# Two heads in one value product of the first attention, a gate unit in its middle, and the meta levels beside the substitution

## The chip, the cores and the metric

One core of a Trainium2 chip runs the whole program. The time is the device time of one execution in microseconds (us), the median of several. TensorE (PE in the profile) multiplies, with the loading of its stationary operand in a row of its own (PEld); VectorE (DVE), ScalarE (ACT) and GpSimd (POOL) do the elementwise work; SyncE (SP) and the queue of GpSimd start transfers. Each engine takes its instructions strictly in the order in which they are written, and semaphores tie the engines together.

## What is computed

Two transformer blocks over 256 tokens of 1024 features. The first prepends 16 meta tokens, projects them once, and runs two branches side by side: a gated delta rule (GDN, 8 heads, chunks) and a sparse attention (DSA, 8 query heads on 2 key heads, the 64 best keys of each query). Both are gated, merged, projected, and followed by an MLP. The second block has a modulated differential attention, a Fourier branch and 16 routed experts. The change touches only these two pieces of the first block:

```python
# GDN, per head and chunk: a triangular inverse, and what it is applied to
A = tril(einsum(k*beta, k) * decay, -1)
Tm = solve_triangular(A + I, I)
attn = einsum(q, k) * decay;  q_dec = q * exp(gc);  g_last = exp(gc[-1])
# DSA, per block of 128 queries and head
p = softmax(where(chosen and causal, q @ k.T * 128**-0.5, -inf))
o = p @ v
merged = sigmoid(gate_a) * (y_gdn @ w_bg) + sigmoid(gate_b) * (y_dsa @ w_bd)
```

## The kernel before

Everything is written by hand, engine by engine, in raw order; no scheduler moves anything. Weights stream in units of 1 MB (128 x 8 x 256 fp32) through a ring of six slots (`ring`, `weight_order`). A dense product is `split_tiles`: ScalarE copies the unit to a rounded type (`w_high`, two buffers, `highs`, L1475), VectorE subtracts that from the unit (`ring_low`, `lows`, L1923), and TensorE does 48 matmuls of 256 columns (L670, L671, L676). `after_unit(kind, u)` stands in the programs of ScalarE and of VectorE where they prepare the unit two places behind the one named: its copy may start only when the unit before it in the same `w_high` buffer has been used. Eight PSUM banks are taken in rotation (`take`); a bank is taken again when its reader has freed it.

**The head loop and the substitution (GDN).** For each of 8 heads TensorE fills three banks: `GB` (the cumulated decay, and beta spread over columns), `KQ` (k·k and k·q) and `TR` (transposes of k and v). VectorE's `decay_args` (L2025) writes the exponents, ScalarE exponentiates them (L1588, L1589) into `scr[:, h % 2]`, and VectorE's `decay_use` masks them (L2035), copies the last column to `egl` (L2036), makes `attn` (L2039), `low` (L2040, L2043) and the decayed q (L2041). ScalarE then makes `k_tail` and `v_beta` from `TR` (L1596, L1597). `decay_args(h)` waits until `TR` of head h-2 is freed by ScalarE, and the exponents of head h-1 are used behind it. Between the heads stand the four meta levels, an inverse of one 128x128 system by doubling: per level one product P (`level_p`, L787), a copy out by ScalarE (`product_out`), one or two products Q and QT (`level_q`, L797, L802) and an update by VectorE (`update_inverse`, L2052 to L2057), each waiting for the one ahead. GpSimd masks the input of each level (L1409) and clears `inv` and `invT` (L1401, L1402) when the last `GB` is filled.

Behind the last head VectorE runs the substitution: four transposes (L2082), 15 steps of two small operations (L2093, L2095), four scalings and eight transposes back (L2107), after which `blocks_ready` lets the remaining twelve levels start on TensorE. TensorE meanwhile has units `mod` 6 and 7 and the two fillers `gz` 0 and 1 (L632, 64 matmul instructions).

**The first attention (DSA).** 16 items `ATT`, first the eight heads of query block 0 (144 keys), then those of block 1 (272 keys). Per item n: logits on TensorE (`att_logits`, L950), mask and maximum on VectorE (L2256, L2258), exponent on ScalarE (L1678), reciprocal and scaling on VectorE (L2265, L2267), transposes on TensorE (`att_transpose`, L958), copy out by ScalarE (L1687, L1688), value product on TensorE (`att_values`, L632, 128 columns, one matmul for each tile of keys), and copy out (L1458) with, for block 1, the rounded copy (L1694) and its remainder on VectorE (L2270). TensorE's order is logits n+1, transposes n-1, values n-3. VectorE's order in item n is mask and maximum of n, then reciprocal and scaling of n-1. Ahead of the transposes stands gate unit `gate_b` 0, and behind the attention the rest alternates, `bd` 0, `gate_b` 1, `bd` 1, `gate_b` 2, ...

## Time and profile before

| what | value |
|---|---|
| three runs | 1255.33, 1258.56, 1259.81 us, median 1258.56 |
| the profiled execution | 1259.38 us, its span 1257.6 us |
| TensorE busy | 1191.4 us, 95% of the span, mean granted clock 0.976 |
| VectorE, ScalarE, GpSimd busy | 667.8, 502.1, 83.9 us |
| the chain that ended last | TensorE 87%, VectorE 9%, ScalarE 2% |

The span is the time from the first to the last recorded instruction; 1.8 us of the execution lie outside it. A row of the timeline says when an instruction began, how long it took, and in brackets how long its engine had sat idle and who ended that. Instructions of one engine overlap in their first and last part, so the next may begin before the one ahead has ended; what a step costs on an engine is the distance between two starts.

### The profile page before, as it was taken

The page shows a single profiled execution, that of the slowest core. Times are in us where ns is not written, and L with a number is a line of the kernel's source. Part 1 is how long each engine was busy: PE and PEld are TensorE (multiplying, and loading weights), DVE is VectorE, ACT ScalarE, POOL GpSimd, SP SyncE. Part 2 cuts the span into 40 slices and gives each one's busy share as a digit, 9 for nine tenths or more (in the row PEclk, how much of TensorE's full clock was granted, in tenths as well). Part 3 has the DMA queues.
Part 4 walks back from the last instruction along what each step waited for, and adds up shares of the span by engine and source line. Part 5 has one row for each costly group of instructions (what it writes and reads, how often), then busy time and mean ns, then how long its engine had stood idle before and what let it go on. Part 6 is the DMA issues. An engine that isn't in the chain of part 4 may idle for free.

```text
span 1257.6 us, 21686 instructions
## 1 busy us (share of the span) xinstructions
PE 1191.4 (95%) x9068; PEld 1027.9 (82%) x9068; DVE 667.8 (53%) x1161; ACT 502.1 (40%) x809; POOL 83.9 (7%) x80
## 2 busy tenths in 40 slices
PE   7999779999899989999998999999899899999996
PEld 6998669998879969999997889966799866666665
DVE  5776685487966565664646332576556441122223
ACT  4775322554355455554344222466533301011112
POOL 2541113000000000000000000000001100000000
PEclk8999889999999999999998999999999899999999
DMA  9546030153422655554554522300865989999980
GB/s 363 189 146 243 13 135 1 68 172 130 163 106 101 239 198 212 191 188 165 184 186 154 196 101 71 132 33 6 326 234 219 387 365 420 420 420 420 420 346 34
DMA packets 36206, 254.61 MB, mean 202 GB/s; under 512 B 4048, under 2 KB 4192, under 8 KB 5904
## 3 DMA queue, kind: packets, MB, share of 16 engines
q1 hardware_dynamic: 33552, 237.83, 49.1%
q0 software_dynamic: 2560, 15.42, 3.1%
q8 instruction: 72, 1.18, 0.4%
q14 instruction: 22, 0.18, 0.0%
HBM read 252.19 MB, written 1.05 MB: 201 GB/s over the span
## 4 chain that ended last, share of the span: by engine, by line
PE 87%; DVE 9%; ACT 2%; issue 2%; DMA 0%; DVEq 0%; ACTq 0%
PE bank L1255 14%; PE bank L676 12%; PE bank L670 12%; PE bank L671 12%; PE bank L632 9%; PE bank L1016 5%; PE bank L1065 4%; PE bank L1023 2%; PE bank L714 1%; PE bank L1274 1%; PE bank L689 1%; PE bank L787 1%; PE bank L802 1%; DVE ring_low L1923 1%; DVE rB L1904 1%
## 5 line engine op out<-in xcount | busy, mean ns | idle before, releaser
L1923 DVE TENSOR_TENSOR ring_low<-ring,w_high 128x2048 fp32r<-128x2048 f32 x104 | 237.9, 2289 | 175.5 <-ACT w_high L1475 175.2
L1475 ACT ACTIVATE w_high<-ring 128x2048 fp32r<-128x2048 f32 x104 | 199.4, 1917 | 311.7 <-PE bank L676 222.3
L670 PE MATMUL bank<-nT_high,w_high 128*128 128x256 f32 (+1 forms) x448 | 115.3, 296 | 0.0
L670 PEld LDWEIGHTS bank<-nT_high,w_high 128*128 128x128 f32 x448 | 85.0, 190 | 2.6 <-issue 2.4
L1255 PE MATMUL bank<-more,xs 128*64 128x256 f32 x768 | 84.5, 379 | 0.0
L670 PE MATMUL bank<-hcl,w_high 128*128 128x256 f32 (+1 forms) x288 | 81.9, 316 | 2.2 <-DVE hcl L2367 2.2
L1255 PEld LDWEIGHTS bank<-more,xs 128*64 128x64 f32 x768 | 55.1, 137 | 29.8 <-issue 2.9
L671 PE MATMUL bank<-hcl,w_high 128*128 128x256 f32 (+1 forms) x288 | 79.4, 307 | 0.0
L670 PE MATMUL bank<-nMs,w_high 128*128 128x256 f32 x256 | 65.2, 292 | 2.0 <-DVE nMs L2312 2.0
L671 PE MATMUL bank<-nT_low,w_high 128*128 128x256 f32 (+1 forms) x272 | 65.5, 282 | 0.0
L671 PE MATMUL bank<-nMs,w_high 128*128 128x256 f32 x256 | 64.8, 291 | 0.0
L1016 PE MATMUL bank<-up,w_high 128*128 128x256 f32 x512 | 64.2, 283 | 0.0
L1016 PEld LDWEIGHTS bank<-up,w_high 128*128 128x128 f32 x512 | 62.5, 192 | 0.1
L670 PEld LDWEIGHTS bank<-hcl,w_high 128*128 128x128 f32 x288 | 55.2, 192 | 7.7 <-issue 4.7
L676 PE MATMUL bank<-nT_high,ring_low 128*128 128x256 f32 (+1 forms) x448 | 59.1, 284 | 1.1 <-DVE ring_low L1923 1.1
L671 PEld LDWEIGHTS bank<-hcl,w_high 128*128 128x128 f32 x288 | 55.2, 192 | 3.5 <-issue 1.0
L676 PEld LDWEIGHTS bank<-nT_high,ring_low 128*128 128x128 f32 x448 | 56.2, 188 | 1.5 <-DVE ring_low L1923 1.5
L670 PEld LDWEIGHTS bank<-nMs,w_high 128*128 128x128 f32 x256 | 51.2, 200 | 2.6 <-issue 2.5
L671 PEld LDWEIGHTS bank<-nT_low,w_high 128*128 128x128 f32 x272 | 52.0, 191 | 1.5 <-issue 1.4
L671 PEld LDWEIGHTS bank<-nMs,w_high 128*128 128x128 f32 x256 | 51.2, 200 | 0.0
L1871 ACT ACTIVATE yb_high<-bank,gate_slot 128x512 fp32r<-128x512 f32 x18 | 12.4, 687 | 82.0 <-PE bank L1255 76.0
L676 PE MATMUL bank<-hcl,ring_low 128*128 128x256 f32 (+1 forms) x288 | 44.4, 307 | 0.0
(542 smaller groups left out, 2490.9 us busy)
## 6 DMA issues: line engine op xcount, KB each, us to landing
ring<-stream SPq DMA_DIRECT2D x163, 1024.0 KB, 4.9
more<-stream SPq DMA_DIRECT2D x60, 1024.0 KB, 16.4
more<-stream POOLq DMA_DIRECT2D x10, 1024.0 KB, 15.3
c<-constants_one SPq DMA_DIRECT2D x1, 1653.0 KB, 16.2
qc<-h_in SPq DMA_DIRECT2D x4, 272.0 KB, 3.8
c<-constants_two POOLq DMA_DIRECT2D x1, 1056.0 KB, 9.4
beside<-stream POOLq DMA_DIRECT2D x1, 1024.0 KB, 12.2
hT<-h_in POOLq DMA_DIRECT2D x1, 1024.0 KB, 5.9
```

Of the source, the lines that this page charges most:

```text
L632: last = nc.tensor.matmul(dst, lhs, rhs, start=(i == 0), stop=(i == len(pairs) - 1))
L670: nc.tensor.matmul(into[j], w, high_x(k), start=first, stop=False, skip_group_check=True)
L671: nc.tensor.matmul(into[j], w, low_x(k), start=False, stop=False, skip_group_check=True)
L676: last = nc.tensor.matmul(into[j], low_w[:, k, j * 128:(j + 1) * 128], high_x(k), start=False, stop=(k == KT - 1), skip_group_check=True)
L689: last = nc.tensor.matmul(dst[rows, 0:UNIT_COLS], silu_c[:, k, :], by_k(s)[:, k, :], start=(k < 4), stop=(k >= 4))
L714: last = nc.tensor.matmul(psum[banks.at[name]][:, 0:n], ones, src[:, k, :], start=(k == 0), stop=(k == KT - 1), skip_group_check=True)
L1016: nc.tensor.matmul(dst[:, j * SEQ:(j + 1) * SEQ], high_w[:, k, j * 128:(j + 1) * 128], up[:, kg * KT + k, part, :], start=(kg == 0 and k = ...
L1023: last = nc.tensor.matmul(dst[:, j * SEQ:(j + 1) * SEQ], low_w[:, k, j * 128:(j + 1) * 128], up[:, kg * KT + k, 0, :], start=False, stop=( ...
L1065: return nc.tensor.matmul(dst[tp][:, j * 256:(j + 1) * 256], hcl[:, 2 * tp + part, k, j * 128:(j + 1) * 128], w[:, k, :], start=first, sto ...
L1255: last = nc.tensor.matmul(dst[rows, :], stationary[:, k, rows], w[j][:, k, :], start=(k == 0), stop=(k == n_k - 1))
L1475: A(w_high[:, d % 2, :], ring[:, s, :], ACT.Copy).then_inc(high_ready, 1)
L1923: TT(ring_low[:, s, :], ring[:, s, :], w_high[:, d % 2, :], sub).then_inc(low_ready, 1)
```

## The change

In the GDN part, the four meta levels leave the head loop on TensorE, ScalarE and VectorE. TensorE does them after the heads, between `mod` 6, `mod` 7 and quarters of the two fillers (`quarter`), ScalarE's `product_out` 0 to 3 stand among the copies of these, and VectorE's updates 0 to 2 stand inside the substitution (behind its first transposes, behind step 9, behind the last step). The copy to `egl` and the decayed q move from VectorE's `decay_use` to GpSimd, which does them for all eight heads behind its second level mask and ahead of clearing `inv` and `invT`.

In the DSA part the transposes of heads 2p and 2p+1 go into one bank (for block 1 into two), ScalarE copies them out as a pair, one value product has 256 columns, and y is copied out and split by pairs. TensorE does the values of pair p at n = 2p + 4. `prob` has four buffers. The order of the weights becomes `gate_b` 0, `gate_b` 1, `bd` 0, `bd` 1, `gate_b` 2, ...; gate unit 1 is multiplied at n = 8, in the middle of the attention, and `after_unit` of gate units 0 and 1 (which prepare `bd` 0 and `bd` 1) stand at n = 5 and n = 13 in both ScalarE's and VectorE's loop.

```diff
-    for u in range(4):
+    order += [("gate_b", 0), ("gate_b", 1), ("bd", 0), ("bd", 1)]
+    for u in range(2, 4):
         order += [("gate_b", u), ("bd", u)]
...
-                if h % 2 == 1:
-                    level_p(h // 2)
-                elif h >= 2:
-                    level_q(h // 2 - 1)
...
             mod_unit(6)
+            level_p(0)
             mod_unit(7)
-            level_q(META_LEVELS - 1)
+            level_q(0)
+            quarter(0, 0)
+            quarter(0, 1)
+            level_p(1)
+            quarter(0, 2)
+            level_q(1)
+            quarter(0, 3)
+            level_p(2)
+            quarter(1, 0)
+            level_q(2)
+            quarter(1, 1)
+            level_p(3)
+            quarter(1, 2)
+            level_q(3)
+            quarter(1, 3)
...
+                if n == 2:
+                    for h in range(H):
+                        pool.wait_ge(decay_exp_ready, h + 1)
+                        pool.wait_ge(*banks.full_when[("KQ", h)])
+                        nc.gpsimd.tensor_copy(egl[:, 2 * h:2 * h + 2], scr[:, h % 2, 256:512].rearrange("p (a b) -> p a b", b=128)[:, :, 127])
+                        nc.gpsimd.tensor_tensor(qc[:, h, META:T], qc[:, h, META:T], scr[:, h % 2, 256:512], mul).then_inc(gpsimd_product, 1)
...
                 step(TT(split(dt, 128), split(dt, 128), over(upper, 2), mul))
-                step(CP(egl[:, 2 * h:2 * h + 2], split(scr[:, h % 2, 256:512], 128)[:, :, 127]))
...
-                step(TT(qc[:, h, META:T], qc[:, h, META:T], scr[:, h % 2, 256:512], mul))
...
-                done(("ao", n), group(dst[:, 0:128], [(av[0:m, i, g * 128:(g + 1) * 128], probT[0:m, n % 2, i * 128:(i + 1) * 128])
+                done(("ao", p), group(dst[:, 0:256], [(av[0:m, i, g * 128:(g + 1) * 128], probT[0:m, p % 2, i, :])
...
-                if n == 0:
-                    second_gate(0)
+                if n % 8 == 0 and n < len(ATT):
+                    second_gate(n // 8)
                 if 1 <= n <= len(ATT):
                     att_transpose(n - 1)
-                if n >= 3:
-                    att_values(n - 3)
+                if n >= 4 and n % 2 == 0:
+                    att_values((n - 4) // 2)
...
+                if n == 5 or n == 13:
+                    after_unit("gate_b", n // 8)
```

The last two added lines stand in ScalarE's loop behind everything else of item n, and in VectorE's behind the maximum of item n and ahead of the reciprocal of item n-1.

On VectorE, in the attention around items 4 to 6, before (the sixth item of block 0 begins with the second `lmask` row):

```order
L2256 SCALAR_TENSOR_TENSOR lmask<-bank,bias 128x144 [waits bank_full1,pexp_ready]
L2258 TENSOR_REDUCE stat<-lmask 128x1 [waits bank_free1]
L2265 RECIPROCAL stat<-stat 128x1 [waits pexp_ready]
L2267 TENSOR_SCALAR prob<-prob,stat 128x144 [waits dve_step]
L2256 SCALAR_TENSOR_TENSOR lmask<-bank,bias 128x144 [waits bank_full4,pexp_ready]
L2258 TENSOR_REDUCE stat<-lmask 128x1 [waits bank_free4]
L2265 RECIPROCAL stat<-stat 128x1 [waits pexp_ready]
L2267 TENSOR_SCALAR prob<-prob,stat 128x144 [waits dve_step]
```

and in the changed kernel:

```order
L2304 SCALAR_TENSOR_TENSOR lmask<-bank,bias 128x144 [waits bank_full0,pexp_ready]
L2306 TENSOR_REDUCE stat<-lmask 128x1 [waits bank_free0]
L2315 RECIPROCAL stat<-stat 128x1 [waits pexp_ready]
L2317 TENSOR_SCALAR prob<-prob,stat 128x144 [waits dve_step]
L2304 SCALAR_TENSOR_TENSOR lmask<-bank,bias 128x144 [waits bank_full2,pexp_ready]
L2306 TENSOR_REDUCE stat<-lmask 128x1 [waits bank_free2]
L1970 TENSOR_TENSOR ring_low<-ring,w_high 128x2048 [waits high_ready]
L2315 RECIPROCAL stat<-stat 128x1 [waits pexp_ready]
L2317 TENSOR_SCALAR prob<-prob,stat 128x144 [waits dve_step]
L2304 SCALAR_TENSOR_TENSOR lmask<-bank,bias 128x144 [waits bank_full4,pexp_ready]
L2306 TENSOR_REDUCE stat<-lmask 128x1 [waits bank_free4]
```

A subtraction `ring_low` of a whole weight unit has come between the maximum of item 5 and the reciprocal of item 4; it waits for ScalarE's rounded copy of the unit. The same stands in item 13.

On GpSimd, behind the masks of the first levels, before:

```order
L1409 TENSOR_TENSOR masked<-metas,c 128x128
L1409 TENSOR_TENSOR masked<-metas,c 128x128 [waits bank_full1] x2
L1401 MEMSET inv 128x2048 [waits bank_full0]
L1402 MEMSET invT 128x2048
L1411 TENSOR_TENSOR masked<-low,c 128x512 [waits bank_full2,bank_free0]
L1411 TENSOR_TENSOR masked<-low,c 128x512 [waits bank_full3]
```

and in the changed kernel (two of the eight heads, then the clearing):

```order
L1435 COPY egl<-scr 128x2 [waits bank_full6,decay_exp_ready]
L1436 TENSOR_TENSOR qc<-qc,scr 128x256
L1435 COPY egl<-scr 128x2 [waits bank_full1,decay_exp_ready]
L1436 TENSOR_TENSOR qc<-qc,scr 128x256
L1438 MEMSET inv 128x2048 [waits bank_full0]
L1439 MEMSET invT 128x2048
L1446 TENSOR_TENSOR masked<-metas,c 128x128 [waits bank_full4,bank_free0]
L1446 TENSOR_TENSOR masked<-metas,c 128x128 [waits bank_full0]
```

The copy to `egl` and the product with `qc` stand once for each head ahead of the clearing of `inv` and `invT`, and the masks of meta levels 2 and 3 behind it.

On TensorE, between the last head and the first of the remaining levels, before:

```order
L787 MATMUL bank<-metas,masked 128x128 [waits bank_free3,bank_free7,masked_ready]
L689 MATMUL bank<-ring,silu_c 32x256 [waits bank_free4,unit_loaded0]
L689 MATMUL bank<-ring,silu_c 32x256 x7
L689 MATMUL bank<-ring,silu_c 32x256 [waits bank_free5,unit_loaded1]
L689 MATMUL bank<-ring,silu_c 32x256 x7
L802 MATMUL bank<-metas,prod 128x128 [waits bank_free6,bank_free3]
L632 MATMUL bank<-nT,ring 128x256 [waits bank_free7,unit_loaded2]
L632 MATMUL bank<-nT,ring 128x256 x15
L632 MATMUL bank<-nT,ring 128x256 [waits bank_free0,unit_loaded3]
L632 MATMUL bank<-nT,ring 128x256 x15
```

and in the changed kernel, from `mod` 6 to the products of level 1:

```order
L690 MATMUL bank<-ring,silu_c 32x256 [waits bank_free3,unit_loaded0]
L690 MATMUL bank<-ring,silu_c 32x256 x7
L788 MATMUL bank<-c,masked 128x128 [waits bank_free4,masked_ready]
L690 MATMUL bank<-ring,silu_c 32x256 [waits bank_free5,unit_loaded1]
L690 MATMUL bank<-ring,silu_c 32x256 x7
L803 MATMUL bank<-c,prod 128x128 [waits bank_free6,bank_free4]
L834 MATMUL bank<-nT,ring 128x256 [waits bank_free7,unit_loaded2]
L834 MATMUL bank<-nT,ring 128x256 x7
L788 MATMUL bank<-metas,masked 128x128 [waits bank_free0,bank_free6,masked_ready]
L834 MATMUL bank<-nT,ring 128x256 x4
L798 MATMUL bank<-prod,metas 128x128 [waits bank_free1,bank_free0]
L803 MATMUL bank<-metas,prod 128x128 [waits bank_free2]
```

Level 0 and 1 of the meta system stand between the modulation units and the quarters of the fillers; two more levels follow in the same way.

## Rows read from the trace of the kernel before

**Rows 1.** The page: the span.

```profile
span 1257.6 us, 21686 instructions
```

**Rows 2.** Windows: stretch, its length, busy us and instructions of each engine, granted clock, DMA.

```profile
183.00:187.00 4.00, 3.93 (x18) 3.96 (x19) 1.42 (x2) 0.67 (x2) 1.18 (x2) 0.50 0.02 4
...
360.20:387.00 26.80, 25.38 (x149) 17.94 (x148) 18.88 (x64) 19.81 (x83) 0.00 (x0) 1.00 0.11 40
```

**Rows 3.** Timeline of VectorE in the head loop, heads 1 and 2.

```profile
127.21 0.61 DVE L2025 TENSOR_SCALAR scr<-bank,tok 128x128 f32<-128x128 f32 x2 [2.30 <-PE bank L810]
...
128.61 0.41 DVE L2040 TENSOR_TENSOR low<-bank,scr 128x256 f32<-128x256 f32 x1
...
130.23 0.61 DVE L2025 TENSOR_SCALAR scr<-bank,tok 128x128 f32<-128x128 f32 x2 [0.40 <-ACT v_beta L1597]
```

**Rows 4.** Timeline of TensorE: a wait of a meta level.

```profile
142.00 0.49 PE L797 MATMUL bank<-prod,metas 128*128 128x128 f32 x2 [1.98 <-ACT prod L1458]
```

**Rows 5.** Timeline of GpSimd: a product of the convolution, and the clearing.

```profile
68.00 2.56 POOL L1395 TENSOR_TENSOR qc<-qc,scr 128x272 f32<-128x272 f32 x1 [1.35 <-ACT scr L1515]
72.75 0.77 POOL L1395 TENSOR_TENSOR qc<-qc,scr 128x272 f32<-128x272 f32 x1 [2.18 <-ACT scr L1515]
...
153.73 1.80 POOL L1401 MEMSET inv<- 128x2048 f32 x1 [16.87 <-PE bank L810]
155.47 1.80 POOL L1402 MEMSET invT<- 128x2048 f32 x1
```

**Rows 6.** Timeline of VectorE: a level's update, and the last two heads.

```profile
152.28 0.29 DVE L2056 TENSOR_TENSOR metas<-metas,bank 128x128 f32<-128x128 f32 x1 [1.26 <-PE bank L797]
...
154.30 0.41 DVE L2035 TENSOR_TENSOR scr<-scr,c 128x256 f32<-128x256 f32 x1
154.64 2.66 DVE L2036 COPY egl<-scr 128x2 f32<-128x2 f32 x1
...
160.20 0.41 DVE L2043 TENSOR_TENSOR low<-low,bank 128x256 f32<-128x256 f32 x1
```

**Rows 7.** Timeline of TensorE beside and behind the substitution.

```profile
163.09 14.01 PE L632 MATMUL bank<-nT,ring 128*128 128x256 f32 x64
183.07 3.75 PE L787 MATMUL bank<-inv,masked 128*128 128x128 f32 x16 [5.98 <-issue]
...
188.60 1.06 PE L787 MATMUL bank<-inv,masked 128*128 128x128 f32 x8
```

**Rows 8.** Timeline of TensorE in the attention: one item of each block.

```profile
365.32 0.41 PE L950 MATMUL bank<-ak,aq 128*128 128x144 f32 x2
...
366.69 0.41 PE L950 MATMUL bank<-ak,aq 128*128 128x144 f32 x2
...
376.39 0.62 PE L950 MATMUL bank<-ak,aq 128*128 128x272 f32 x2
376.85 0.49 PE L958 MATMUL bank<-c,prob 128*16 128x128 f32 x3
377.27 1.12 PE L632 MATMUL bank<-probT,av 16*128 16x128 f32 x6
378.23 0.62 PE L950 MATMUL bank<-ak,aq 128*128 128x272 f32 x2
```

**Rows 9.** Timeline of VectorE in the attention.

```profile
356.28 2.29 DVE L1923 TENSOR_TENSOR ring_low<-ring,w_high 128x2048 fp32r<-128x2048 f32 x1
...
365.84 0.31 DVE L2256 SCALAR_TENSOR_TENSOR lmask<-bank,bias 128x144 f32<-128x144 f32 x1 [0.25 <-PE bank L950]
...
377.12 0.44 DVE L2256 SCALAR_TENSOR_TENSOR lmask<-bank,bias 128x272 f32<-128x272 f32 x1 [0.54 <-PE bank L950]
...
378.14 0.36 DVE L2267 TENSOR_SCALAR prob<-prob,stat 128x272 f32<-128x272 f32 x1
```

**Rows 10.** Timeline of ScalarE: the rounded copies of y and of a unit.

```profile
377.37 0.42 ACT L1694 ACTIVATE y_dsa_high<-y_dsa 128x256 fp32r<-128x256 f32 x1
...
387.95 1.90 ACT L1475 ACTIVATE w_high<-ring 128x2048 fp32r<-128x2048 f32 x1
```

More of the change, by code:

```diff
@@ L822, in _, with quarter @@
                 done(("TR", h), last)
-                if h % 2 == 1:
-                    level_p(h // 2)
-                elif h >= 2:
-                    level_q(h // 2 - 1)
+            placed = {}
+            def quarter(u, q):
+                if q == 0:
+                    placed[u] = unit("gz", u), take(("gz", u))
+                (s, cnt), dst = placed[u]
+                j, half = divmod(q, 2)
+                for k in range(half * KT // 2, (half + 1) * KT // 2):
+                    last = nc.tensor.matmul(dst[:, j * SEQ:(j + 1) * SEQ], by_k(s)[:, k, j * 128:(j + 1) * 128], nT[:, k, META:T],
+                                            start=(j == 0 and k == 0), stop=(k == KT - 1), skip_group_check=True)
+                if q == 3:
+                    last.then_inc(unit_used[s], 1)
+                    banks.full_when[("gz", u)] = (unit_used[s], cnt)
             mod_unit(6)
+            level_p(0)
             mod_unit(7)
-            level_q(META_LEVELS - 1)
-            for kind, u in FILLERS:
-                s, cnt = unit(kind, u)
-                dst = take((kind, u))
-                for j in range(2):
-                    last = group(dst[:, j * SEQ:(j + 1) * SEQ], [(by_k(s)[:, k, j * 128:(j + 1) * 128], nT[:, k, META:T]) for k in range(KT)])
-                last.then_inc(unit_used[s], 1)
-                banks.full_when[(kind, u)] = (unit_used[s], cnt)
+            level_q(0)
[13 more added lines that the diff above has]
+            quarter(1, 3)
             for n in range(META_LEVELS, len(LEVEL_ITEMS)):
@@ L1599, in _ @@
                             ins.then_inc(free(("TR", g)), 1)
-                if h >= 2 and h % 2 == 0:
-                    product_out(h // 2 - 1)
             evac_mod(6)
+            product_out(0)
             evac_mod(7)
-            for u in range(2):
-                gz_out(u)
+            product_out(1)
+            product_out(2)
+            gz_out(0)
+            product_out(3)
+            gz_out(1)
             for n in range(META_LEVELS, len(LEVEL_ITEMS)):
@@ L1656, in second_gate @@
                     emptied(act, ("bg", u + 2))
-                A(gate[:, u % 2, :], full(act, ("gate_b", u))[:, :], ACT.Copy if u == 0 else ACT.Sigmoid).then_inc(free(("gate_b", u)), 1)
+                A(gate[:, u % 2, :], full(act, ("gate_b", u))[:, :], ACT.Copy if u < 2 else ACT.Sigmoid).then_inc(free(("gate_b", u)), 1)
             first_gate(0)
@@ new lines, in _ @@
+                    A(prob[:, n % 4, 0:nkeys(qt)], lmask[:, n % 2, 0:nkeys(qt)], ACT.Exp, bias=stat[:, n % 2, 0:1],
+                      accum_out=stat[:, n % 2, 1:2]).then_inc(pexp_ready, 1)
+                if n >= 3 and n % 2 == 1 and n < len(ATT) + 3:
+                    p = (n - 3) // 2
+                    qt, h = ATT[2 * p]
+                    bank = full(act, ("pt", p))
+                    if p >= 2:
+                        act.wait_ge(*banks.full_when[("ao", p - 2)])
+                    if qt == 0:
+                        step(A(probT[0:META, p % 2, 0, :], bank[0:META, 256:512], ACT.Copy))
+                        A(probT[:, p % 2, 1, :], bank[:, 0:256], ACT.Copy).then_inc(free(("pt", p)), 1)
+                    else:
+                        A(probT[:, p % 2, 1:3, :], bank[:, :].rearrange("p (a b) -> p a b", b=256), ACT.Copy).then_inc(free(("pt", p)), 1)
+                        A(probT[0:META, p % 2, 0, :], full(act, ("pt_meta", p))[0:META, 0:256], ACT.Copy).then_inc(free(("pt_meta", p)), 1)
@@ L2260, in _ @@
                     after_unit("bg", 3)
+                if n == 5 or n == 13:
+                    after_unit("gate_b", n // 8)
                 if n >= 1:
```

105 lines of the change are left out of this document (57 added, 48 removed).

## The prediction

> **What bounds the kernel.** I read the page first, for the span [rows 1] and for TensorE, which is busy for almost all of it. A change can therefore gain in two ways: less work on TensorE, or less of the little that it waits. So I went to the two stretches that the diff touches, by windows and then by the timelines of each engine. In the attention, 360.2 to 387.0, TensorE has 25.4 of 26.8 us of work at the full granted clock [rows 2]: it is the bound there. In the head loop it waits for ScalarE's copy of a meta level's product, 1.98 us at 142.00, one of three such waits [rows 4]. Behind the loop VectorE alone sets the pace: from the end of its last `low` at 160.61 [rows 6] to the first of the remaining levels at 183.07, before which TensorE had sat idle for 5.98 us [rows 7].
>
> **The head loop.** Where no level stands between, a head takes 3.02 us (VectorE's `decay_args` at 127.21 and at 130.23, the second released by ScalarE's `v_beta`) [rows 3]. The reader is to see a ring: exponents on VectorE, `low` 1.40 behind them, ScalarE's four copies, the next exponents. The changed loop is this ring alone. Of what moves to GpSimd, the product with q stands behind `low` and off the ring, so it saves nothing; the small copy stands inside, but the operation behind it has to await the mask's end in any case, so I count 0.1. Six rings of 2.92 behind 127.21 put the exponents of head 7 at 127.21 + 6 x 2.92 = 144.7. The use of head 6 (0.53 until it begins, then 1.5) and that of head 7 (1.55) end at 148.3. Against 160.61 that is 12.3.
>
> **GpSimd's part.** For each head a copy of two columns and a product of 256, for which the convolution's product of 272 columns shows 0.77 alone and 2.56 where it met VectorE [rows 5]. I take 0.77, plus at most 0.3 for the copy, which fits in 2.92; it starts some 1.4 behind the exponents, when VectorE is at operations that read PSUM. Only the last head has no exponents of a later one ahead of it, so there VectorE's mask (L2035) meets the product: 0.4. Behind it the clearing comes at once, 3.6 us. A price for that stands in rows 6: the small copy took 2.66 us because it arrived within the clearing [rows 5] and was served at its end. If the mask of head 7 were held like that, it would cost 3.6. But L2035 at 154.30, wholly within the same clearing, took its ordinary 0.41 [rows 6]. I take 0.4 and keep 3.6 as the far end.
>
> The Trainium skill ("SBUF — State Buffer", section "Who interferes with whom") says that a VectorE instruction with two SBUF inputs contends with a GpSimd one that reads SBUF, not with one that only writes, and that a copy in a two-port mode contends with either. By that rule the mask would be held by the product and not by the clearing. The copy at 154.64 and the mask at 154.30 agree.
>
> **Levels beside the substitution.** VectorE gets three updates more, each two operations of 0.29 with a wait between [rows 6]: 3 x 0.57 = 1.7. The substitution itself stays 22.5 (160.61 to 183.07). TensorE's work beside it is the fillers (14.0), the two modulation units (3.3) and some 2 for the levels, plus one round trip through ScalarE of about 2 at level 0: done 21 to 24 after 144.5, when VectorE still has 4 or 5 to go. So these waits are covered; if they weren't, the last filler would end later than VectorE, which takes another 5. The sum: 12.3 - 0.4 - 1.7 = **10.2 less**, ends 6.5 (clearing holds the mask) and 12 (updates hidden, nothing met). Everything behind it (levels, scan, dense units) is bound by TensorE or by VectorE's own chain and moves along; no unit is waited for there, since the stream runs ahead.
>
> **The attention: work saved.** In block 1 an item takes 1.84: logits 0.46, transposes 0.42, values 0.96 [rows 8]; in block 0 it takes 1.37. A matmul instruction of 256 columns costs 14.01 / 64 = 0.219 [rows 7], and a product is two of them (six for three tiles [rows 8]). A pair's values cost 6 x 0.219 = 1.31 in place of 1.92, and in block 0 4 x 0.219 = 0.88 in place of about 1.5. Over 4 + 4 pairs: 4.8 less.
>
> **Given back to the chain.** From the start of an item's logits VectorE begins 0.73 later (376.39, 377.12) and ends scaling the item before at 378.50 [rows 8, 9]: the transposes can start 2.1 behind the logits. Before, TensorE had 0.46 + 0.42 + 0.96 + 0.46 = 2.30 in between, so the chain was just hidden. Now values come at every second item only; in the item without them there are 0.46 + 0.42 + 0.46 = 1.34, and TensorE waits 0.7. In block 0, with 0.52 from logits to VectorE [rows 8, 9], it is 0.8. I lay the items out by these numbers: waits of 0.4 and 0.8 in block 0, three of 0.7 in block 1, the rest covered by the gate unit in the middle or the tail; 3.3, of which 0.3 was there before. Net of the two paragraphs: 1.8 less. Gate unit 1 costs what it did (5.8), only earlier.
>
> **The conversions in the middle.** This is the term that I weigh most. Before, the attention held no conversion but the one in item 1 (2.29 at 356.28 [rows 9], under gate unit 0's matmuls), and the next (1.90 at 387.95 [rows 10]) ran under `bd` 0. Now ScalarE does one behind everything of items 5 and 13, and VectorE's subtraction waits for it ahead of the reciprocal of the item before. What stands behind it on VectorE is the scaling of `prob` 4 (or 12), which TensorE's next transposes need; behind those nothing of TensorE can pass. TensorE has one logits product to do and then idles: the exponent (0.4), two pair copies (0.5), the copy of y (0.3), 1.90, 2.25 and the reciprocal and scaling (0.4) make 5.8 from VectorE's maximum (the small ones estimated from the same timeline); without the insertion 0.8 would pass until the transposes. The stall at item 5 is 5.0. At item 13 the copies are longer (0.5, 0.5, 0.3, 0.4, and 0.5 for the rounded copy of a pair, which was 0.42 for one head [rows 10]): 5.5. Of the 10.5 I let 0.9 be saved in shorter waits next to them: 9.6 more. What would hide it is a dense unit on TensorE; gate unit 1 stands at item 8, three items behind the first stall and five ahead of the second. If that cover were there, the term would be nothing.
>
> **The clock.** After the 5.98 idle, the first 16 matmuls took 3.75 us at a granted 0.50, the lower level, where 8 take 0.9 later [rows 2, 7]: 1.9 lost. Two stalls of 5 us should do likewise. Some of it falls in the chain's waits; I take 1.5 each, 3 in all, ends 0 and 4.
>
> **Sum.** -10.2 - 1.8 + 9.6 + 3.0 = +0.6. The attention with gate unit 1, 26.8 + 5.8, becomes 43.4. The profiled execution of before (1259.4, span 1257.6) lies 0.8 above the median; on the median the sum gives 1258.6 + 0.6 = 1259.2, and I say **1259.5**.
>
> **Rivals.**
> 1. *Faster: the stalls at items 5 and 13 don't show.* This would be if VectorE and ScalarE stood items ahead of TensorE. Then 12.6 go away: 1247. Against it, one logits product is all that TensorE gives ahead, and `lmask` has two buffers; the row at 377.12 follows its logits at once. Chance 0.09.
> 2. *The clearing holds the last head's mask*, 3.6 of the gain: 1262.8. The copy's 2.66 speaks for it, the mask's 0.41 against. 0.10.
> 3. *The half clock lasts longer* than after the idle row, through the four or five items behind each stall, where nearly all is on TensorE: 2 more each, 1263.5. 0.10.
> 4. *Slower: GpSimd becomes the bound of the head loop.* If its copy and product take more than the ring's 2.92 (the product alone 2.56 as at 68.00 [rows 5], the copy 0.7 or more), ScalarE's exponents of head h wait for the product of h-2 and the loop takes GpSimd's pace; it decides from 3.7 on, where 7 x 0.8 = 5.6 are lost: 1265 and more. Against it, at 68.00 it met a subtraction of 2.29, and in the loop the longest two-input operation takes 0.41. 0.08. The other side of the page's rule, that each product and each mask of a head stop one another, is this rival in small: 0.4 a head, 3 in all, within the range.
>
> The forecast, about equal sums, has the remaining 0.63. A measurement of this kernel can tell about 0.5%, 6.3 us, from no change. Faster by more is rival 1, 0.09, and a little of the forecast's spread, 0.10 in all; slower is rival 4 and the joint upper ends, 0.12; within is 0.78. The range takes in rivals 2 and 3 and, below, a gain of 12 with a clock that costs nothing: 1254 to 1265.
>
> **What would show it.** GDN: `decay_args` of the heads about 2.9 apart, L2043 of head 7 near 148.5, the first of the remaining levels near 173, three updates inside the substitution. VectorE's mask of head 7 at 0.4 or at 4 tells rival 2; GpSimd's product at 0.8 or 2.5 tells rival 4. Attention: two idle rows of TensorE of 5.0 and 5.5 ended by VectorE's `prob`, each behind a `w_high` and a `ring_low`; waits of 0.7 in every second item; value products in rows of 0.88 and 1.31; a granted clock of 0.50 behind each stall. I am wrong if the stretch from `gate_b` 0's last matmul to `bd` 0's first is under 38 or over 46, or if the GDN gain is under 7.

## The result and the profile after

The changed kernel takes **1266.89 us** (median of 9 runs, 1262.19 to 1269.55), the kernel before 1258.56 (7 runs, 1255.33 to 1259.81): ratio 1.0064, 95% interval 1.0048 to 1.0080. It is slower by some 8 us, where 1259.5 and a range up to 1265 were forecast. The profiled spans are 1265.0 and 1257.6 [rows 1]: 7.4 us, which the account below has to give. Runs that a second, slower condition of the chip disturbed are left out of every median and ratio here.

**The GDN part gained.** VectorE in the changed kernel: the exponents of heads 1, 2 and 7, the mask and `low` of head 7, and the substitution (start, duration, engine, line, operation, idle time before it and who ended that).

```profile
127.54 0.61 DVE L2072 TENSOR_SCALAR scr<-bank,tok 128x128 f32<-128x128 f32 x2 [2.42 <-PE bank L811]
...
130.48 0.61 DVE L2072 TENSOR_SCALAR scr<-bank,tok 128x128 f32<-128x128 f32 x2 [0.76 <-ACT v_beta L1636]
...
145.19 0.61 DVE L2072 TENSOR_SCALAR scr<-bank,tok 128x128 f32<-128x128 f32 x2 [0.76 <-ACT v_beta L1636]
...
147.29 0.44 DVE L2082 TENSOR_TENSOR scr<-scr,c 128x256 f32<-128x256 f32 x1
...
148.56 0.42 DVE L2088 TENSOR_TENSOR low<-low,bank 128x256 f32<-128x256 f32 x1
...
160.21 0.22 DVE L2139 TENSOR_TENSOR state<-state,root 128x55 f32<-128x55 f32 x1
160.70 1.14 DVE L2139 TENSOR_TENSOR state<-state,root 128x48 f32<-128x48 f32 x1
```

Heads 1 to 7 now begin 2.94 us apart (forecast: 2.92), heads 2 to 7 each released by ScalarE's `v_beta`; the last `low` starts at 148.56 where it stood at 160.20 [rows 6]. The mask of the last head, at 147.29, took 0.44.

GpSimd at the same place, and TensorE where the remaining levels begin:

```profile
146.59 0.19 POOL L1435 COPY egl<-scr 128x2 f32<-128x2 f32 x1 [2.08 <-ACT scr L1628]
146.73 0.73 POOL L1436 TENSOR_TENSOR qc<-qc,scr 128x256 f32<-128x256 f32 x1
147.39 1.80 POOL L1438 MEMSET inv<- 128x2048 f32 x1
...
160.69 1.09 POOL L1448 TENSOR_TENSOR masked<-low,c 128x512 f32<-128x512 f32 x1 [4.31 <-PE bank L788]
```

```profile
173.60 3.56 PE L788 MATMUL bank<-inv,masked 128*128 128x128 f32 x16 [5.19 <-issue]
```

The levels begin at 173.60, 9.47 earlier than at 183.07 [rows 7]; 10.2 was forecast. A part of the missing 0.7 stands in the rows: GpSimd's mask at 160.69 reads two SBUF operands, and VectorE's subtraction of the substitution that began with it took 1.14, where the same 48 columns took 0.21 before (at 171.54). The two traces can be compared here because their head loops begin at nearly the same place (exponents of head 0 at 124.30 and 124.52); in most other executions of this study that place is 121.9 to 122.0, so the position of one row in two traces tells a gain only to some 2.5 us, and distances within a trace tell it better: from there to the first of the levels 58.8 before and 49.1 now. The gain arrives unspent at the attention, whose first logits start at 350.53 instead of 360.20.

**The attention lost more than that.** TensorE in the changed kernel, from the first logits behind gate unit 0 (the matmuls of the gate units left out):

```profile
350.53 0.41 PE L970 MATMUL bank<-ak,aq 128*128 128x144 f32 x2
350.77 0.38 PE L985 MATMUL bank<-c,prob 128*16 128x128 f32 x2
350.99 0.41 PE L970 MATMUL bank<-ak,aq 128*128 128x144 f32 x2
352.14 0.38 PE L985 MATMUL bank<-c,prob 128*16 128x128 f32 x2 [0.74 <-DVE prob L2317]
...
353.38 0.38 PE L985 MATMUL bank<-c,prob 128*16 128x128 f32 x2 [0.61 <-DVE prob L2317]
...
354.25 0.39 PE L985 MATMUL bank<-c,prob 128*16 128x128 f32 x2 [0.24 <-DVE prob L2317]
354.56 2.25 PE L633 MATMUL bank<-probT,av 16*128 16x256 f32 x4
356.61 0.69 PE L970 MATMUL bank<-ak,aq 128*128 128x144 f32 x2
361.90 0.59 PE L985 MATMUL bank<-c,prob 128*16 128x128 f32 x2 [4.61 <-DVE prob L2317]
...
373.96 1.32 PE L633 MATMUL bank<-probT,av 16*128 16x256 f32 x4
375.12 0.62 PE L970 MATMUL bank<-ak,aq 128*128 128x272 f32 x2
...
379.33 0.49 PE L985 MATMUL bank<-c,prob 128*16 128x128 f32 x3
379.65 0.62 PE L970 MATMUL bank<-ak,aq 128*128 128x272 f32 x2
381.03 0.50 PE L985 MATMUL bank<-c,prob 128*16 128x128 f32 x3 [0.75 <-DVE prob L2317]
381.46 1.75 PE L633 MATMUL bank<-probT,av 16*128 16x256 f32 x6
383.05 0.62 PE L970 MATMUL bank<-ak,aq 128*128 128x272 f32 x2
389.03 0.80 PE L985 MATMUL bank<-c,prob 128*16 128x128 f32 x3 [5.37 <-DVE prob L2317]
```

What VectorE did in the first of the two long gaps, with the release by ScalarE's rounded copy of the unit:

```profile
359.06 2.29 DVE L1970 TENSOR_TENSOR ring_low<-ring,w_high 128x2048 fp32r<-128x2048 f32 x1 [4.30 <-ACT w_high L1512]
361.27 0.16 DVE L2315 RECIPROCAL stat<-stat 128x1 f32<-128x1 f32 x1
361.46 0.29 DVE L2317 TENSOR_SCALAR prob<-prob,stat 128x144 f32<-128x144 f32 x1
```

The same stretch in windows (length; busy us and instructions of TensorE, its weight loads, VectorE, ScalarE, GpSimd; granted clock; DMA):

```profile
350.53:354.80 4.27, 2.68 (x19) 1.87 (x18) 3.38 (x14) 2.50 (x10) 0.00 (x0) 0.99 0.65 232
354.80:368.70 13.90, 9.29 (x28) 6.17 (x28) 6.07 (x16) 5.75 (x15) 0.00 (x0) 0.51 0.01 5
368.70:388.90 20.20, 13.46 (x82) 10.12 (x80) 8.37 (x22) 9.13 (x22) 0.00 (x0) 1.00 0.16 53
388.90:395.70 6.80, 6.67 (x20) 4.30 (x20) 3.70 (x12) 2.98 (x8) 0.00 (x0) 0.50 0.00 0
```

Both stalls are there, 4.61 and 5.37 (forecast 5.0 and 5.5), each behind a `ring_low` that waited for its `w_high`. The reader is to see two things that the forecast did not have. The value product of a pair takes 1.16 us from start to start in block 0 (373.96 to 375.12) and 1.59 in block 1 (381.46 to 383.05), not 0.88 and 1.31. And the half clock begins at about 354.8, 2.5 us before the first stall, and lasts nearly 14 us (the stall of 4.61 is inside it); with the second stretch of it, it is 20.7 us of the 48.3 from 350.53 to the first matmul of `bd` 0 at 398.83. Before, the same work took 26.84 + 5.8 = 32.6. The loss of 15.7 here is 6.0 more than the 9.67 gained ahead of it, and the span ends 7.4 later.

One saving is smaller and easy to overlook. From the start of an item's transposes to what follows them, TensorE takes 0.42 in block 1 when a value product follows [rows 8] and 0.31 in block 0 (365.64 to 365.95 before), but 0.32 and 0.22 when logits follow (379.33 to 379.65, 350.77 to 350.99). Fourteen such steps led to a value product before, seven do now: 0.6 saved in all.

### The profile page after: what moved, and what is told of

It is laid out like the page before. It is cut to its first block, busy times and chain, and to the rows that moved or that the text cites. A ratio compares the mean times of both kernels' runs of the same rounds, so it can differ in the third digit from the quotient of the medians.

```text
span 1265.0 us, 21561 instructions
## 1 busy us (share of the span) xinstructions
PE 1193.2 (94%) x9028; PEld 1027.4 (81%) x9028; DVE 662.8 (52%) x1141; ACT 501.6 (40%) x781; POOL 90.8 (7%) x96
## 4 chain that ended last, share of the span: by engine, by line
PE 86%; DVE 9%; ACT 2%; issue 2%; DMA 0%; DVEq 0%; POOL 0%; ACTq 0%
PE bank L1287 14%; PE bank L671 12%; PE bank L677 12%; PE bank L672 12%; PE bank L633 8%; PE bank L1048 5%; PE bank L1097 4%; PE bank L1055 2%; PE bank L715 1%; PE bank L1306 1%; DVE ring_low L1970 1%; PE bank L834 1%; PE bank L788 1%; PE bank L803 1%; PE bank L690 1%
```

## The experiments

In the diffs the unmarked changed kernel is the base, but for the first two, whose base is the kernel before. The kernel before, beside them, took 1257.6, 1258.1, 1259.0 and 1257.7 us (medians of 16, 16, 10 and 12 runs). "Stretch" is always from the first logits behind gate unit 0 to the first matmul of `bd` 0, gate unit 1 included where it lies inside, and a "dip" is a stretch in which the granted clock was 0.50.

### Each half of the change alone

```diff
# the GDN part alone: the head loop, the levels beside the substitution,
# GpSimd's copy and product; the attention as before
+            level_p(0)
             mod_unit(7)
+            level_q(0)
+            quarter(0, 0)
...
# the attention alone: the rest of the change on the kernel before
+    order += [("gate_b", 0), ("gate_b", 1), ("bd", 0), ("bd", 1)]
```

> The kernel of before with only the GDN part of the change. Theory (the two parts add up, and what the head loop and the substitution save, 9.5 us in the trace of the changed kernel, reaches the end): 1249 to 1250 us, ratio to before about 0.9925, the first of the remaining levels at 173.6. Rival (the earlier start is given back behind it, in a wait for weights or in VectorE's choice of keys): 1254 or more, with a new wait between 220 and 350.

> The kernel of before with only the attention part. Theory (all the loss is made between the last matmul of gate unit 0 and the first of bd 0, 15.6 us there): 1274 us, ratio 1.0125. Rival (the attention costs only the 10.8 that was forecast, and the rest of the loss is an interplay with the GDN part, such as where the clock's dips fall): 1269 us.

The GDN part alone: 1248.6 us (3 runs), ratio 0.9896 (0.9796 to 0.9996); the same kernel once more, beside the later ones:

> The GDN part of the change alone, once more, beside the version with the pieces on one chip: 1249 to 1250, 9 below before. If the pieces' version is faster by its account, it is so by the value products' fixed part (2.6) and the covered waits: 2 to 3 us.

Measured: ratio 0.9927 (0.9909 to 0.9944), three executions of 1248.4 to 1250.8. The attention alone: 1274.07, ratio 1.0104 (1.0024 to 1.0184), stretch 47.6. The medians give -9 and +16, and the changed kernel's +8 is their sum within the noise (the interval of the attention alone is wide, 3 to 23 us); its stretch is long without the GDN part too, so the loss is the attention's. Its stalls there were 4.85 and 5.37.

The clock in this trace tells something more. The short waits of the first items are those of the changed kernel (0.74, 0.60 and 0.24), yet the clock stayed full behind them and fell only within the stall, which began at 361.08:

```profile
360.00:362.00 2.00, 1.09 (x5) 0.68 (x4) 0.00 (x0) 1.91 (x6) 0.00 (x0) 1.00 0.00 0
362.00:372.00 10.00, 6.07 (x18) 4.12 (x19) 5.71 (x15) 3.29 (x9) 0.00 (x0) 0.52 0.01 2
```

### The conversions moved under gate unit 1 and behind the attention

```diff
-                if n == 5 or n == 13:
-                    after_unit("gate_b", n // 8)
+                if n == 8:                      # VectorE: n == 9, behind the scaling
+                    after_unit("gate_b", 0)
+            after_unit("gate_b", 1)             # behind the loop
```

> The changed kernel, but the conversion of bd 0 stands at item 8 (ScalarE) and behind item 9's scaling (VectorE), under gate unit 1's matmuls, and that of bd 1 behind the attention, under bd 0. Theory (the two conversions and the half clock that follows them are the loss): no idle row of TensorE above 1 us, the stretch from gate_b 0 to bd 0 falls from 48.3 to 33 to 34 us and the time to 1252 us. Rival (the waits in every second item alone bring the half clock, since the first dip began at 354.7, ahead of the first stall): a granted clock of 0.50 remains somewhere in the attention, the stretch is 36 to 40 us and the time 1255 to 1259 us.

1255.23 us (10 runs, 1248.33 to 1258.33), ratio 0.9978 (0.9959 to 0.9997), stretch 36.6. No idle row of TensorE in the attention is longer than 0.75. The stalls were the conversions'. But the clock still fell, and stretch and time are the rival's:

```profile
348.65:353.00 4.35, 2.77 (x19) 1.93 (x18) 3.45 (x16) 2.57 (x10) 0.00 (x0) 1.00 0.66 222
353.00:363.10 10.10, 9.80 (x31) 6.81 (x30) 4.70 (x17) 5.05 (x15) 0.00 (x0) 0.50 0.03 11
```

Ahead of the dip TensorE was busy for 2.77 of 4.35 us, with waits of 0.74, 0.61 and 0.23; the dip itself is almost full of work at half speed.

### Extra matmuls in the gaps

TensorE multiplies operands that stand ready into a bank that the next product overwrites; nothing else waits for these.

```diff
+                for i in range({1: 10, 2: 4, 3: 2, 4: 36, 12: 40}.get(n, 0)):
+                    w = 128 if n in (1, 3) else 256
+                    nc.tensor.matmul(main[:, 384:512] if w == 128 else main[:, 0:256],
+                                     nT_high[:, i % KT, META:META + 128], nT_high[:, i % KT, META:META + w], start=True, stop=True)
                 pe.wait_ge(prob_ready, n + 1)
```

All five places filled:

> The changed kernel, but TensorE does matmuls whose result is overwritten while it waits: 10 short ones, 4 and 2 ahead of the transposes of items 1 to 3, 36 ahead of item 4, 40 ahead of item 12 (36 x 0.117 = 4.2 and 4.7 us, both less than the stalls of 4.6 and 5.4). Nothing else differs, so the stalls stay and only the clock can change. Theory (the loss beyond the forecast is mostly the half clock, which reached over 14 us at the first stall and 7 at the second): full clock throughout, about 6 us less, 1260 to 1261 us. Rival (the half clock costs the 3 us forecast, since much of it lies in waits): 1264 us.

1259.48 us (10 runs), ratio 1.0010 (0.9999 to 1.0021), 7.4 less than the changed kernel (6.8 by the ratios); the granted clock was 1.00 in every window of the stretch, which took 42.0. The waits of VectorE and ScalarE are all still there, only covered (TensorE still stood for 0.50 and 0.56 behind the fillings of items 4 and 12). So the half clock costs the attention at least 6.3 us; behind the two fillings new waits of 0.32 and 0.33 show, which the slower work at half clock had covered. Only items 1 to 3 (counts 10, 4, 2):

> The changed kernel with the extra matmuls ahead of items 1 to 3 alone; the two long stalls stay. It tells what brings the half clock of the changed kernel, which began at 354.8, ahead of the first stall. Theory A: the short waits began it and the stall prolonged it. Filled, the clock is 1.00 up to the stall and 0.50 only for some 5 to 7 us behind it, as at the second stall; the stretch goes from 48.3 to about 45.5 and the time from 1266.9 to about 1264. Rival: the stall would bring the same loss by itself, and the dip only shifts: 48 us and 1266 to 1267. If all of the loss came from the short waits, 42 to 43 and 1260.

1268.57 us, ratio 1.0084 (1.0067 to 1.0101), stretch 48.1: nothing gained. The dip now began in the stall (1.00 in the window 351 to 355, 0.50 from 357 on) and lasted until about 366. The rival was right: the stall brings it by itself. Only items 4 and 12 (36 and 40):

> The changed kernel with the extra matmuls in the two long stalls (36 ahead of the transposes of item 4 and 40 ahead of those of item 12) and none in items 1 to 3. Both together brought the stretch from 48.3 to 42.0 us and the time from 1266.9 to 1259.5; those of items 1 to 3 alone brought nothing. Theory A: the short waits and the stall each bring the clock down by themselves, and one stretch of half clock is paid whichever brings it. Then only the second stall's loss (3.1) goes, and in the first half the waits of items 1 to 3 keep 0.50 for some 10 us, as in the kernel with the first conversion under gate unit 1: stretch 45 to 46, time 1263 to 1264. Rival: the stalls are the whole cause, and without them the short waits bring no half clock here: stretch 42, time 1259.5.

1261.71 us (10 runs), ratio 1.0025 (1.0013 to 1.0036), stretch 43.9: 2.2 over the kernel with all filled. The short waits brought 0.50 from 354.7 to 361.3:

```profile
354.70:361.30 6.60, 6.60 (x27) 5.77 (x27) 2.41 (x3) 3.10 (x6) 0.00 (x0) 0.50 0.03 7
361.30:394.26 32.96, 30.56 (x191) 24.07 (x190) 16.47 (x47) 16.31 (x43) 0.00 (x0) 1.00 0.10 33
```

The size was below what I expected: the dip lasted 6.8 us, where I had assumed 10, and a part of it fell on the extra matmuls themselves. Last, items 1 to 3 filled in the kernel with the conversions moved:

> The kernel with the first conversion under gate unit 1 and the second behind the attention, and 10, 4 and 2 extra matmuls of TensorE on operands that stand ready (their results are overwritten) ahead of the transposes of items 1 to 3, where it waited 0.74, 0.61 and 0.24. Theory A: those short waits alone brought the clock to 0.50 for 10 us. Filled, the granted clock stays at 1.00, the stretch goes from 36.6 to 33.5 and the time from 1255.2 to 1252. Rival: the clock is not what made these items slow, but VectorE and ScalarE did; then the stretch stays at 36 and the time at 1255.

1249.72 us, ratio 0.9927 (0.9910 to 0.9943), stretch 32.5 (36.6 without them), clock 1.00 throughout. With the conversions hidden and the clock kept, the attention of the change takes what it took before (32.6), and the time is that of the GDN part alone: what the pairs save (2.6 in the products, 0.6 in the steps above) their waits give back (4.6, filled or not, where 1.4 had been [rows 2]).

### Pairs alone

The order of the weights, gate unit 1 and both conversions as before; only pairs of heads.

```diff
-    order += [("gate_b", 0), ("gate_b", 1), ("bd", 0), ("bd", 1)]
-    for u in range(2, 4):
+    for u in range(4):
...
-                if n % 8 == 0 and n < len(ATT):
-                    second_gate(n // 8)
+                if n == 0:
+                    second_gate(0)
...
-                if n == 5 or n == 13:
-                    after_unit("gate_b", n // 8)
```

> The changed kernel with the pairs of heads, but the order of the weights, the second gate unit and both conversions where the kernel before has them. So the only new things in the attention are the products of 256 columns and the waits in every second item. Theory A: a pair saves only the fixed 0.30 us of one product (0.32 in block 0, 0.33 in block 1, 2.6 in all), the waits give 3.0 back, and the waits of the first items bring the granted clock to 0.50 for about 10 us, which costs some 3. The stretch from the last matmul of gate unit 0 to the first of bd 0 is then 26.8 - 2.6 + 3.0 + 3 = 30 us, and the time about 3.5 over that of the GDN part alone (1249.8): 1253. Theory B: the half clock comes only with a long stall near by; then the stretch is 27.2 and the time 1250. The forecast's own price of a product (4.8 saved, full clock) would give 25.0 and 1248.

1255.55 us (10 runs, 1248.72 to 1258.98), ratio 0.9976 (0.9962 to 0.9991), stretch 32.4 instead of 26.8. The profiled execution held 0.50 from about 352 to 366, and its waits were 0.74, 0.60, 0.24, 0.30, 0.33, 0.76 and 0.75. By its terms 26.8 - 2.6 - 0.6 + 3.7 - 1.4 (the idle time of before [rows 2]) is 25.9; the other 6.5 is put down to the clock by difference, since no run filled these waits. Theory A had the mechanism and too small a size. This kernel and the one with the conversions moved each had one of ten executions at 1248.7 and 1248.3, with a mean clock of 0.978 and 0.979 where the others had 0.969 to 0.975. No trace of these two was kept; they look like executions without the dip, as the trace of the attention alone is one.

### Gate unit 1 in pieces

```diff
+            PIECES = {1: 4, 2: 6, 4: 5, 6: 5, 8: 6, 10: 6, 12: 5, 14: 5, 16: 6}
...
-                if n % 8 == 0 and n < len(ATT):
-                    second_gate(n // 8)
+                if n == 0:
+                    second_gate(0)
+                gate_piece(PIECES.get(n, 0))    # so many of the unit's 48 matmuls
...
+                if n in (4, 6, 8, 10):          # ScalarE; VectorE in 5, 7, 9, 11
+                    A(w_high[:, d % 2, 512 * q:512 * q + 512], ring[:, sl, 512 * q:512 * q + 512], ACT.Copy)
```

> The changed kernel with gate unit 1 cut into nine pieces of 4 to 6 matmuls (48 in all), one ahead of the transposes in each item in which no value product stands (and one in item 1), the conversion for bd 0 cut into four pieces of 512 columns (ScalarE behind items 4, 6, 8, 10, VectorE behind 5, 7, 9, 11), and the one for bd 1 behind the attention. Theory A: the waits of the pairs are a matter of order alone. With 0.6 us of dense work in each they vanish, as does the half clock; the stretch is 26.8 + 5.8 - 2.6 = 30 to 31 us (48.3 in the changed kernel) and the time 1247 to 1248, less than the GDN part alone (1249.8). Rival: the chain of VectorE and ScalarE, with the pieces of the conversion in it, is what paces the items; then the waits stay in part, 33 to 34 us, and the time is 1250 to 1252.

1255.04 us, ratio 0.9971 (0.9960 to 0.9982): a miss, by an error of mine in the order. On VectorE I had put the subtraction for `bd` 1 ahead of the remainders of y, and `bd` 0 waited for it:

```profile
383.81 0.55 PE L674 MATMUL bank<-y_dsa_high,w_high 128*128 128x256 f32 x1 [5.96 <-DVE y_dsa_low L2372]
```

With that order mended:

```diff
-            after_unit("gate_b", 1)
             for p in range(H // 2):
                 dve.wait_ge(y_dsa_high_ready, p + 1)
                 ...
+            after_unit("gate_b", 1)
```

> The kernel with gate unit 1 in nine pieces, but VectorE's subtraction for bd 1 behind the remainders of y and not ahead of them, where it held bd 0 for 5.96 us and brought the half clock for 5.4 us behind. Theory A: with both gone, bd 0 begins at about 378 and the time is 1255.0 - 5.9 - 2 = 1246 to 1248. Rival: TensorE then waits 3 or more at bd 1 for its conversion, which ends about 4.5 us behind the last copy of y; since bd 0 takes 5.8, I give that at most 1: 1248.

1245.23 us, ratio 0.9897 (0.9883 to 0.9912). The stretch is 28.7 (348.29 to 376.99), 3.9 below before, and what waits are left are these:

```profile
351.14 0.38 PE L988 MATMUL bank<-c,prob 128*16 128x128 f32 x2 [0.34 <-DVE prob L2355]
...
355.29 0.39 PE L988 MATMUL bank<-c,prob 128*16 128x128 f32 x2 [0.16 <-DVE prob L2355]
...
366.25 0.49 PE L988 MATMUL bank<-c,prob 128*16 128x128 f32 x3 [0.17 <-DVE prob L2355]
...
370.44 0.49 PE L988 MATMUL bank<-c,prob 128*16 128x128 f32 x3 [0.17 <-DVE prob L2355]
```

The pairs' 3.2 and 0.6 less waiting (0.84 against 1.42) give 3.8 of the 3.9. So the pairs do save what their fixed parts come to, once the same dense work that stood in one block at item 8 lies under the waits.

### The fixed part of a value product

```diff
-                                                      for i, (a, m) in enumerate(key_tiles(qt))]))
+                                                      for i, (a, m) in list(enumerate(key_tiles(qt)))[::-1]]))
```

> The mended version with the key tiles of each value product in reverse order, the tile of 16 meta keys last. Every value product of this case costs a fixed 0.30 us beside 0.107 for each instruction of 128 columns or 0.215 for one of 256. Theory A: the 0.30 is the step from 16 rows to 128 within the product (the weight load of the second tile comes 0.33 late behind the 16-row one); with the small tile last it shrinks to 0.1 or less, 1.6 us in all over eight products. Rival: it belongs to the step from the transposes to the product; then the rows stay at 1.16 and 1.59 and the time does not change.

The base is the mended version. TensorE's weight loads of one product of block 1, the base first:

```profile
366.68 0.29 PEld L636 LDWEIGHTS bank<-probT,av 16*128 16x128 f32 x2 [0.17 <-DVE lmask L2344]
367.30 0.73 PEld L636 LDWEIGHTS bank<-probT,av 128*128 128x128 f32 x4 [0.33 <-issue]
```

```profile
367.32 0.73 PEld L636 LDWEIGHTS bank<-probT,av 128*128 128x128 f32 x4
368.38 0.29 PEld L636 LDWEIGHTS bank<-probT,av 16*128 16x128 f32 x2 [0.33 <-issue]
```

The load is 0.33 late at the change between 16 and 128 rows, in either direction, and only the 0.17 at the start of the product goes away: a product's row shrinks from 1.75 to 1.65 us. From start to start a product takes 1.58 instead of 1.59 (367.43 to 369.01, 366.68 to 368.27 in the base), since the change back to 128 rows now falls on the logits behind it, and the stretch is 28.7 as in the base. The time, 1248.34 us, ratio 0.9917 (0.9902 to 0.9932), is no better. Theory A falls as to the size: within a product the step between tiles of different height is there anyway. That it belongs to the step from the transposes, as the rival had it, is not shown either.

### The idle row ahead of the remaining levels

```diff
+                if n == META_LEVELS:            # ahead of the wait of the first remaining level
+                    dst = take(("P", n))
+                    for i in range(22):         # then: range(11)
+                        nc.tensor.matmul(dst[:, 0:SEQ], nT[:, i % KT, META:META + 128], nT[:, i % KT, META:T], start=True, stop=True)
```

> The mended version with 22 extra matmuls of 256 columns (results overwritten) behind the last quarter of the fillers, where TensorE sat idle for 5.2 us ahead of the first of the remaining levels and then ran 3.6 us of it at 0.50. Theory: the clock stays at 1.00, the row of 16 matmuls takes about 1.9 in place of 3.75, and the time falls by 1.7 to 1.9 against the mended version: 1244.5 to 1246. Rival: the levels are paced by ScalarE and VectorE there and the gain is lost in the next waits: no change.

1247.76 us, ratio 0.9915 (0.9902 to 0.9928), slower than its base. I had counted 0.22 us for a multiplication; it is two instructions of that length in this type, and the row was twice as long as the gap. With half of them:

> The version with the pieces, with 11 extra multiplications (22 matmul instructions of 0.219 us, 4.8 us in all) in the idle 5.2 us ahead of the first of the remaining levels; with twice as many they took 9.66 us and the levels began late, but the first sixteen instructions then took 1.80 from start to start in place of 3.54. Theory: the levels begin as early as before and at full clock, and the time falls by 1.7 from 1245.2: 1243.5. Rival: the next levels wait for ScalarE and VectorE instead, and nothing is gained: 1245 to 1246.

1243.55 us (4 runs), ratio 0.9876 (0.9849 to 0.9902), the fastest kernel of the study, though its interval overlaps that of its base. TensorE with 22 and with 11:

```profile
168.00 9.66 PE L787 MATMUL bank<-nT 128*128 128x256 f32 x44
177.50 1.95 PE L796 MATMUL bank<-inv,masked 128*128 128x128 f32 x16
```

```profile
166.30 4.91 PE L787 MATMUL bank<-nT 128*128 128x256 f32 x22
171.81 2.02 PE L796 MATMUL bank<-inv,masked 128*128 128x128 f32 x16 [0.60 <-DVE invT L2199]
173.69 1.16 PE L806 MATMUL bank<-prod,invT 128*128 128x128 f32 x8
```

The sixteen instructions take 1.88 from start to start, 3.34 in the changed kernel and 3.54 in the base of this one (171.11 to 174.65): 1.5 to 1.7 is what the half clock costs there. The levels begin 0.7 later than in the base, so a part of it is given back.

## Why the prediction was wrong

Told in its own order; the forecast was +0.6 to the profiled span, measured +7.4.

1. **Head loop and levels: right, 0.7 too much.** Forecast -10.2, measured -9.5. The ring of 2.92 was 2.94, the mask of the last head took 0.44 (rival 2, the clearing, is out), GpSimd's copy and product took 0.19 and 0.73 and never 2.56 (rival 4 is out). What I had not priced is that GpSimd's masks of the next levels now fall on the substitution: 0.9 at 160.70 and 0.2 at 156.03. Against that, the three updates took about 1.0 instead of the 1.7 put down for them, and the last `low` ended at 148.98, where the forecast comes to 148.7: 1.1 - 0.7 + 0.3 is the 0.7. The Trainium skill ("SBUF — State Buffer", "Who interferes with whom") names just this pair, a GpSimd operation that reads SBUF against a VectorE one with two SBUF inputs; the rows at 160.69 and 160.70 agree, and so does the undisturbed mask beside the clearing. I had applied the rule only to the operations that the change moved, not to those that it moved them beside.

2. **Work saved by pairs: mis-sized, 1.6.** Forecast -4.8, which set six or four instructions of 0.219 against the whole of two old products. The rows of before already held the rest: 0.96 for six instructions and about 0.74 for four are 0.11 each and a fixed 0.30. The new ones, 1.59 and 1.16, are 0.215 each and the same 0.30. The columns are as many as before; only one fixed part in two goes, eight times 0.32 or 0.33, so the products save 2.6, and with the 0.6 of the steps from transposes, which I had not seen, 3.2. I took a price per instruction from one kind of row and a price per product from another, and put the difference down as a gain.

3. **Waits given back: right in place.** In block 1 two of 0.75 where 0.7 was forecast (the third fell into the second stall), in block 0 0.74, 0.61 and 0.24 for 0.4 and 0.8: 3.1 in all. TensorE had idled for 1.4 us before [rows 2], of which I had counted 0.3, so net they cost 1.7, not 3.0.

4. **Conversions in the middle: right.** Forecast stalls of 5.0 and 5.5, net 9.6; measured 4.61 and 5.37, 10.0. Moving the conversions took both away. Rival 1 is out.

5. **The clock: the step that failed.** Forecast 3.0, "two stalls of 5 us", 1.5 each, with 0 and 4 as its ends; measured 6.3 by filling the gaps. Two errors lie in it. The price came from one place where 16 instructions followed an idle row in unbroken work. In the attention the half clock went on for 13.9 and 6.8 us, through items that hardly wait, so that most rows in it are nearly twice as long. That was rival 3, which I gave 0.10 and 2 us a stall; its 3 + 4 is about what was measured. Its 1263.5 is still 3.4 below the median, and the pairs' 1.6 is the largest part of that. And I looked for the cause in long stalls alone. The waits of the first items can suffice: without any idle row over 0.75 the clock stood at 0.50 for 10 and 14 us, and it cost 4.1 (measured by filling them) and 6.5 (by difference) of the two stretches. Before, waits of 0.74 and 0.52 in the same place had passed at full clock [rows 2].

The attention's sum is then 32.6 - 3.2 + 1.7 + 10.0 + 7.2 = 48.3 as measured, against 43.4 forecast and over the 46 that the prediction had named as the sign of being wrong; 7.2 is what the first four leave to the clock, and the filling gave 6.3, or 6.95 with the two waits that the half clock had covered. With 0.5 less gain at the attention's start than forecast, 5.4 of the 6.8 between forecast and measurement are placed. The remaining 1.4 appears in small steps between `bd` 0 and the end, 0.4 by the first matmul of `wo` and 1.1 from there to TensorE's last one (822.5 before, 823.6 now). The two traces of the GDN part alone, one and the same kernel, differ by 2.6 in that last distance (825.4 and 822.8), so the 1.1 is no more than one execution differs from another; the 0.4 stays open. So does what decides whether a series of short waits brings the clock down: behind the same three waits it fell in four traces (the changed kernel, the conversions moved, pairs alone, items 4 and 12 filled) and stayed full in that of the attention alone.

## What to carry to other kernels

This fusion, which halves the number of products, saved their fixed parts and no columns: split a row of n and a row of 2n instructions into slope and constant before pricing it. Where an engine at its bound gets a new rhythm, price each short wait twice, once for its length and once for the clock that a dense stretch behind it may lose; cutting a dense unit into pieces of 0.5 to 0.8 us and laying them under the waits removed most of the waits and the dip here (36.6 to 28.7 us, the stalls being gone in both), where the same unit in one block at item 8 covered none of the short waits. Conversions and other long elementwise work go where the engine that waits for them has dense work of its own, and in pieces if it has none.

## What the runs showed of the hardware

- With TensorE busy for 2.8 of 4.35 us, with waits of at most 0.74 between, the granted clock went from 1.00 to 0.50 (2.4 to 1.2 GHz) and stayed there for 10.1 us of almost unbroken work (9.80 busy); with the waits filled it stayed at 1.00. In one of five traces with these waits it did not fall.
- One idle row of 4.9 us did the same; both together cost no more than one of them, as long as the dips overlap (stretches of 48.1 and 48.3 us).
- In value products of 256 columns a weight load of TensorE came 0.33 us late at the change from 16 to 128 rows, and 0.17 or 0.33 at the change from 128 to 16.
- VectorE's subtraction with two SBUF inputs took 1.14 instead of 0.21 us beside a GpSimd multiplication of 128x512, and an operation beside GpSimd's clearing was not held.
